# Weights rounded one block ahead in the heads, and the second block's attention values computed token-wise

## The reference

```python
# first block: 8 recurrent heads of 128 and 16 attention heads of 64
z = u @ w_in
hq, hf, hi, hg, aq, ak, av, gates = jnp.split(z, SPLIT_POINTS, axis=-1)
q = jax.nn.silu(hq) * (HG_DK ** -0.5)          # g = lb + (1 - lb) * sigmoid(hf)
o = rms_norm(hgrn2_scan(q, 1 - g, hi, log_g), hg_norm_w) * jax.nn.silu(hg)
ya = chunk_band_attention(aq, ak, av, rel_bias)
merged = gate_a * (y_a @ w_branch_a) + gate_b * (y_b @ w_branch_b)

# second block: 8 gMLP groups of 128 and 16 neighbourhood attention heads of 64
proj = h @ w_in
uv, qkv, gates = jnp.split(proj, [2 * GM_WIDTH, 2 * GM_WIDTH + 3 * NA_WIDTH], axis=-1)
y_a = gmlp_branch(uv, ln_g, ln_b, w_s, b_s)    # u * (w_s mixed over tokens of layernorm(gelu(v)) + b_s)
y_b = neighbourhood_attn(q, k, v, rpb)
```

## Time and profile before

| what | us |
|---|---|
| median of the runs | 2853.17 |
| the profiled execution | 2853.04 |
| its span in the trace | 2851.2 |
| TensorE busy in the span | 2815.1 (99%) |
| VectorE busy | 2162.9 (76%) |
| ScalarE busy | 1511.7 (53%) |
| GpSimd busy | 130.7 (5%) |
| moved by DMA | 521 MB, 183 GB/s over the span |

### The profile page before, as it was taken

How to read it: one execution, slowest core, us unless ns; L and a number is a source line. 1 busy time by engine, 2 the same in 40 slices (tenths; PEclk the granted TensorE clock), 3 DMA queues, 4 the chain that set the end, 5 groups by cost and what they waited for, 6 DMA issues and landing times.

```text
span 2851.2 us, 42194 instructions
## 1 busy us (share of the span) xinstructions
PE 2815.1 (99%) x16058; PEld 2422.3 (85%) x16058; DVE 2162.9 (76%) x3239; ACT 1511.7 (53%) x2248; POOL 130.7 (5%) x121
## 2 busy tenths in 40 slices
PE   9999999999999999999999999999999999999998
PEld 6888888888888888888888888888888888888887
DVE  5688877888777777777787766668768878777876
ACT  5555665656544444444465555546555555555554
POOL 0010000100100000000040000000010000000002
PEclk9999999999999999999999999999999999999999
DMA  7544554445555555555665565655556655555553
GB/s 267 180 146 153 167 160 156 157 159 184 192 190 192 184 193 186 188 193 183 194 213 189 172 192 161 197 174 186 189 180 190 196 190 187 190 192 187 189 188 123
DMA packets 157305, 521.23 MB, mean 183 GB/s; under 512 B 28976, under 2 KB 31408, under 8 KB 156976
## 3 DMA queue, kind: packets, MB, share of 16 engines
q1 hardware_dynamic: 155952, 516.26, 55.8%
q10 hardware_dynamic: 1152, 2.27, 0.2%
HBM read 516.37 MB, written 2.10 MB: 182 GB/s over the span
## 4 chain that ended last, share of the span: by engine, by line
PE 83%; DVE 11%; ACT 3%; issue 3%; DMA 0%; DVEq 0%; ACTq 0%; SPq 0%
PE acc L371 32%; PE acc L376 16%; PE psT L371 9%; PE psX L371 9%; PE psT L376 4%; PE psX L376 4%; DVE w_lo L1162 4%; ACT w_hi L733 2%; DVE HS L1303 1%; PE acc_first L371 1%; DVE work L1168 1%; DVE HS L1312 1%; PE acc L406 1%; PE acc L405 1%; PE acc L404 1%
## 5 line engine op out<-in xcount | busy, mean ns | idle before, releaser
L1162 DVE TENSOR_TENSOR w_lo<-w_raw,w_hi 128x1024 fp32r<-128x1024 f32 (+1 forms) x960 | 1171.1, 1226 | 368.1 <-ACT w_hi L733 342.1
L733 ACT ACTIVATE w_hi<-w_raw 128x1024 fp32r<-128x1024 f32 (+1 forms) x960 | 1000.4, 1052 | 435.2 <-PE acc L371 213.5
L371 PE MATMUL acc<-XU,w_hi 128*128 128x512 f32 x2784 | 904.5, 397 | 0.5 <-DVE work L1168 0.5
L371 PE MATMUL acc<-XY,w_hi 128*128 128x512 f32 x2208 | 715.4, 398 | 0.0
L376 PEld LDWEIGHTS acc<-XU,w_lo 128*128 128x128 f32 x2784 | 523.0, 188 | 121.7
L376 PE MATMUL acc<-XU,w_lo 128*128 128x256 f32 x2784 | 547.5, 278 | 0.0
L376 PEld LDWEIGHTS acc<-XY,w_lo 128*128 128x128 f32 x2208 | 414.9, 188 | 96.9 <-DVE XY L1350 1.1
L371 PEld LDWEIGHTS acc<-XU,w_hi 128*128 128x128 f32 x2784 | 436.0, 189 | 6.6 <-issue 2.7
L376 PE MATMUL acc<-XY,w_lo 128*128 128x256 f32 x2208 | 434.5, 278 | 0.8 <-DVE XY L1350 0.8
L371 PEld LDWEIGHTS acc<-XY,w_hi 128*128 128x128 f32 x2208 | 344.2, 189 | 8.6 <-issue 5.8
L738 ACT ACTIVATE cross<-acc 128x256 f32<-128x256 f32 x246 | 93.6, 380 | 238.1 <-PE acc L371 238.0
(11 more groups left out here) (295 smaller groups left out, 2972.0 us busy)
## 6 DMA issues: line engine op xcount, KB each, us to landing
w_raw<-in_weights SPq DMA_DIRECT2D x956, 512.0 KB, 3.5
bias<-in_rel_bias SPq DMA_DIRECT2D x8, 384.0 KB, 3.3
bias<-in_rpb_back SPq DMA_DIRECT2D x32, 96.0 KB, 6.7
w_raw<-in_weights SPq DMA_DIRECT2D x8, 384.0 KB, 3.0
hT<-in_x_t SPq DMA_DIRECT2D x8, 256.0 KB, 8.5
G<-in_norm_rows SPq DMA_DIRECT2D x1, 1024.0 KB, 7.6
out_dram<-G SPq DMA_DIRECT2D x2, 512.0 KB, 3.7
out_dram<-G ACTq DMA_DIRECT2D x2, 384.0 KB, 4.7
```

The source lines that it names most:

```text
L371: return nc.tensor.matmul(bank[:, :], hi[:, k, col:col + P], X[:, k0 + k, :], start=first and k == 0, stop=last and k == nk - 1 and k % 2 ...
L733: act.activation(w_hi[s][:, 0:n], w_raw[s][:, 0:n], ACT.Copy).then_inc(hi_done, 1)
L1162: V.tensor_tensor(w_lo[s][:, 0:n], w_raw[s][:, 0:n], w_hi[s][:, 0:n].bitcast(F32), ALU.subtract).then_inc(lo_ready, 1)
```

## The change

**Rounding.** In both head phases ACT rounds one block ahead of where its program stood: a new `round_next(p, i, b)` rounds what `round_block` for b+1 would (at the end of an iteration the next iteration's first, at the end of the phase nothing), and one `round_block(p, 0, 0)` stands ahead of the loop. In `heads1` it comes right after `copy_cross` in odd blocks, ahead of the block's job, and after the job in even blocks (at b = 0 first). In `heads2` it comes ahead of the jobs in all blocks.

**First heads.** DVE does `softmax_front` at b = 11 and 13 ahead of the tile sum and scaling of the gate tile, no longer behind them. PE does `attend` ahead of `scan_rms` at b = 17.

**Second heads.** The tile av goes out of the heads (14 blocks, 7 tiles); `gmv` has 32 blocks, of which the last 16 make av token-wise in the same banks. ACT copies it, scaled, in pieces of 128 columns to places of their own (`near_value`) at b = 23 and 31, four heads and two token tiles each, and raises `av_out`, for which PE waits at b = 0 and 2 of the first second head. The transposes L476 and the copy L1005 go. The layer-norm steps of the gate values move from the first second head into b = 16 to 21 of `gmv` (their squares now go to `probs`, gain and shift to the start of G). PE's jobs, and ACT's and DVE's steps for them, move up: mix to 5, scores to 6 and 8, transposes to 11, attend to 13. Seven tiles an iteration make bank and cross buffer alternate over iterations (`head2_bank`, `p.cross`). The bias is loaded at b = 4 in place of 6.

The diff, cut to its core (bodies of functions that only move are left out, and so are eight columns of indentation):

```diff
@@ -135,7 +135,7 @@
     ("ffn1last", 1, *ffn_counts("ffn1last"), None),
-    ("gmv", 1, 16, 0, 0, None), ("heads2", HEADS, 16, 8, 8, None),
+    ("gmv", 1, 32, 0, 0, None), ("heads2", HEADS, 14, 7, 7, None),
     ("branch2", 2, 16, 16, 16, None), ("out2", 2, 16, 8, 0, None),
@@ -225,13 +225,22 @@
 val_banks = [[acc[0], acc[1]], [psA, psE]]
-gain, shift = Gf[:, 16 * T:16 * T + WIDTH], Gf[:, 20 * T:20 * T + WIDTH]
+gain, shift = Gf[:, 0:WIDTH], Gf[:, WIDTH:2 * WIDTH]
...
     return G[:, KD + 2 * i + kind, :].rearrange("p (a n) -> p a n", a=NT)
+def near_value(i):
+    if i < 5:
+        return G[:, (8, 9, 12, 16, 20)[i], :].rearrange("p (a n) -> p a n", a=NT)
+    return (AT[:, 0:NT, :], v_nat[:, :, :], av_nat[:, :, :])[i - 5]
+def head2_bank(i, t):
+    return acc[(7 * i + t) % 2]
@@ -323,9 +332,9 @@
             sp.wait_ge(S("mz_ready1"), KD)
-            sp.dma_start(Gf[:, 16 * T:16 * T + 2 * WIDTH],
+            sp.dma_start(Gf[:, 0:2 * WIDTH],
                          bass.AP(tensor=norm_rows.tensor, offset=0, ap=[[0, P], [1, 2 * WIDTH]])).then_inc(S("bs_in"), 16)
-        if name == "heads2" and b == 6:
+        if name == "heads2" and b == 4:
             offset = i * (2 * RPB_R * RPB_C) + RPB_BACK
@@ -460,9 +469,9 @@
                 bank_free(p, i, t)
-            if p.name == "heads1" and i == 0 and b in (0, 2):
-                pe.wait_ge(S("vals_out"), NT * (3 + b // 2))
+            if i == 0 and b in (0, 2):
+                pe.wait_ge(S("vals_out" if p.name == "heads1" else "av_out"), NT * (1 + 2 * (p.name == "heads1") + b // 2))
             products(p, i, b, bank_of(t), X, KB * (b % 2), b % 2 == 0, b % 2 == 1)
@@ -541,8 +550,6 @@
             pe.wait_ge(S(f"probs_ready{x}"), i * 2 + 2)
-            if x == 2:
-                pe.wait_ge(S("av_ready2"), i + 1)
             for h, bank in enumerate((psT, psX)):
@@ -553,7 +560,7 @@
             pe.wait_ge(S(f"pT_ready{x}"), i * 3 + 3)
-            av = head_value(1, i) if x == 1 else av_nat[:, :, :]
+            av = head_value(1, i) if x == 1 else near_value(i)
             for h in range(2):
@@ -580,7 +587,7 @@
         16: [scan_out, prob_transposes(1)],
-        17: [scan_rms, attend(1)],
+        17: [attend(1), scan_rms],
     }
@@ -655,7 +662,10 @@
     for b in range(p.blocks):
-        value_products(p, b, XY, val_banks[b // (KD // 2)], one_by_one(x_ready, KD))
+        c = b // (KD // 2)
+        if b in (KD, 3 * KD // 2):
+            pe.wait_ge(S("gv_ready"), NT * (c - 1))
+        value_products(p, b, XY, val_banks[c % 2], one_by_one(x_ready, KD))
         if b == 3:
@@ -664,7 +674,6 @@
     pe.wait_ge(S("ws_in"), 16)
-    pe.wait_ge(S("gv_ready"), NT)
@@ -680,16 +689,15 @@
     after2 = {
-        6: [mix],
-        7: [scores(0, T, 2)],
-        8: [transpose_pair(wk(5), "avz_ready2", "avT_full2")],
-        9: [scores(1, T, 2)],
-        13: [prob_transposes(2)],
-        15: [attend(2)],
+        5: [mix],
+        6: [scores(0, T, 2)],
+        8: [scores(1, T, 2)],
+        11: [prob_transposes(2)],
+        13: [attend(2)],
     }
...
     for i in range(p.iters):
-        in_tiles(p, i, XY, after2, lambda t: acc[t % 2])
+        in_tiles(p, i, XY, after2, lambda t: head2_bank(i, t))
     branches("branch2")
@@ -735,7 +743,7 @@
         act.wait_ge(w_used, p.block(i, b) + 1)
-        act.activation(cross[:, c % 2, :], bank[:, T:2 * T], ACT.Copy).then_inc(cross_ready, 1)
+        act.activation(cross[:, p.cross(i, c) % 2, :], bank[:, T:2 * T], ACT.Copy).then_inc(cross_ready, 1)
@@ -796,7 +804,15 @@
                 value_tile(b // 8, a)
+    def round_next(p, i, b):
+        if b + 1 < p.blocks:
+            round_block(p, i, b + 1)
+        elif i + 1 < p.iters:
+            round_block(p, i + 1, 0)
     p = ph["heads1"]
+    round_block(p, 0, 0)
@@ -825,21 +841,25 @@
         for b in range(p.blocks):
-            round_block(p, i, b)
             t = b // 2
+            if b == 0:
+                round_next(p, i, b)
             if b % 2:
...
                 copy_cross(p, i, t, b, acc_first if t == 0 else acc[(t - 1) % 2])
+                round_next(p, i, b)
             if b == 1:
...
                 act.activation(wk(0), wk(0), ACT.Ln).then_inc(S("lg_ready"), 1)
+                round_next(p, i, b)
             if b == 3:
...
                 act.activation(lg_hi[:, :, :], psT[:, 0:T], ACT.Copy).then_inc(S("lg_hi_ready"), 1)
+                round_next(p, i, b)
             if b == 5:
@@ -958,6 +981,18 @@
+    def value_squares():
...
+    def value_rstd():
...
     p = ph["gmv"]
@@ -966,52 +1001,47 @@
-        if b % (KD // 2) == KD // 2 - 1:
+        if b == 17:
+            value_squares()
+        if b == 18:
+            value_rstd()
+        if b in (23, 31):
+            act.wait_ge(w_used, p.block(0, b) + 1)
+            for a in range(NT):
+                for h in range(4):
+                    ins = act.activation(near_value(4 * (c - 2) + h)[:, a, :], val_banks[c % 2][a][:, h * P:(h + 1) * P],
+                                         ACT.Copy, scale=tok_rs[:, a:a + 1])
+                ins.then_inc(S("av_out"), 1)
+        if b in (7, 15):
...
-    def value_squares():
...
-    def value_rstd():
...
+    round_block(p, 0, 0)
...
-            round_block(p, i, b)
...
-                copy_cross(p, i, t, b, acc[t % 2])
+                copy_cross(p, i, t, b, head2_bank(i, t))
+            round_next(p, i, b)
...
-            if i == 0 and b == 2:
-                value_squares()
-            if i == 0 and b == 3:
-                value_rstd()
...
-            if b == 8:
-                act.wait_ge(S("avT_full2"), i + 1)
-                act.activation(av_nat[:, :, :], psT[:, 0:T], ACT.Copy).then_inc(S("av_ready2"), 1)
...
+            if b == 11:
+                evac_pT(0, 2, i)
+            if b == 12:
+                evac_pT(1, 2, i)
...
-                evac_pT(0, 2, i)
-            if b == 14:
-                evac_pT(1, 2, i)
-            if b == 15:
@@ -1165,7 +1195,7 @@
         dve.wait_ge(cross_ready, p.cross(i, c) + 1)
-        mark(V.tensor_tensor(dst, bank[:, 0:T], cross[:, c % 2, :], ALU.add), acc_free,
+        mark(V.tensor_tensor(dst, bank[:, 0:T], cross[:, p.cross(i, c) % 2, :], ALU.add), acc_free,
              p.tile(i, t) + 1 + TILE_CREDIT)
@@ -1324,6 +1354,10 @@
                 low_part(p, i, b)
+            if b == 11:
+                softmax_front(0, P, 1, i)
+            if b == 13:
+                softmax_front(1, T, 1, i)
             if b in (11, 13, 15, 17):
@@ -1333,12 +1367,8 @@
                     link(ins)
-            if b == 11:
-                softmax_front(0, P, 1, i)
             if b == 12:
                 softmax_back(0, P, 1, i)
-            if b == 13:
-                softmax_front(1, T, 1, i)
             if b == 16:
@@ -1441,6 +1471,20 @@
+    def value_mean():
...
+    def centre_values(a):
...
+    def scale_values(a):
...
     p = ph["gmv"]
@@ -1448,22 +1492,14 @@
             norms_two()
-        for j in range(2 * b - KD, 2 * b - KD + 2) if b >= KD // 2 else ():
+        if b == 16:
+            value_mean()
+        if b in (18, 19):
+            centre_values(b - 18)
+        if b in (20, 21):
+            scale_values(b - 20)
+        for j in range(2 * b - KD, 2 * b - KD + 2) if KD // 2 <= b < KD else ():
             link(V.scalar_tensor_tensor(hT[:, j, :], hT[:, j, :], cols[:, C_FIN1 + j:C_FIN1 + j + 1], rs1[:, :], ALU.mult, ALU.mult))
-    def value_mean():
...
-    def centre_values(a):
...
-    def scale_values(a):
...
@@ -1472,14 +1508,7 @@
             t = b // 2
-            bank = acc[t % 2]
-            if i == 0 and b == 0:
-                value_mean()
-            if i == 0 and b == 3:
-                centre_values(0)
-                centre_values(1)
-            if i == 0 and b in (4, 5):
-                scale_values(b - 4)
+            bank = head2_bank(i, t)
             if b == 1:
@@ -1502,26 +1531,23 @@
             if b == 7:
-                scaled_tile(p, i, 3, b, 3, bank, wk(5), S("avz_ready2"), i + 1)
                 softmax_front(0, T, 2, i)
-            if b == 8:
-                softmax_back(0, T, 2, i)
             if b == 9:
-                tile_sum(p, i, 4, b, 4, bank, wk(8))
-                link(V.tensor_tensor(G[:, ds(i * 4, 1), :], work[:, 8:9, 0:T], rs[:, :].rearrange("p (a t) -> p a t", a=1), ALU.mult))
                 softmax_front(1, T, 2, i)
-            if b == 10:
-                softmax_back(1, T, 2, i)
-            if b in (11, 13, 15):
-                n = (b - 9) // 2
-                tile_sum(p, i, 4 + n, b, 4 + n, bank, wk(8))
+            if b in (7, 9, 11, 13):
+                n = (b - 7) // 2
+                tile_sum(p, i, 3 + n, b, 3 + n, bank, wk(8))
                 ins = V.tensor_tensor(G[:, ds(i * 4 + n, 1), :], work[:, 8:9, 0:T],
...
                     link(ins)
-            if b == 15:
+            if b == 8:
+                softmax_back(0, T, 2, i)
+            if b == 10:
```

(8 more changed lines are left out.)

30 lines of the change are left out of this document (16 added, 14 removed).

## The result

Before 2853.26 us (median of four runs), after **2828.94 us** (2827.18 to 2829.49, four runs): a ratio of 0.9914, 95% interval 0.9897 to 0.9931. That is 24.3 us less where 21.1 were forecast, and 0.06 us under the stated range, 2829 to 2840.

A forecast was written before the change was run, and what follows sets the result against it. TensorE, busy nearly all the time at full clock, was taken as the bound. From 2853.04 us, -17.3 + 1.0 - 1.1 - 1.9 - 1.8 = -21.1 gave 2831.9, 2832 us against the median; range 2829 to 2840.

The forecast's parts named there:

- Rival (3): First heads: DVE's late work is its own load, not ACT's order, so only -4.8 counts; 2848 us, chance 0.06.
- rival (4): First heads: ACT's new order starves the head start (sigmoids into logarithm and decays); 2853 us and over, chance 0.04.
- rival (2): First heads' tail: DVE stays the limit, block 16's bank or the square replaces old waits; 2840 to 2841, chance 0.10.
- -17.3 us for the two waits: First heads: TensorE's waits at `scan_rms` (8.9 us) and `scan_out` (8.4) both vanish; 0 to 0.3 us a head may remain.
- +1.0 us at `branch1`: Start of `branch1`: the 0.8 us wait for y_a's low part grows by 1.0 us (0 to 2.0).
- The cover at the head's tail: First heads' end: `AT_ready` at 216.7, before TensorE is ready at 217.45; square ready and asked for at 222.7, a tie.
- `gmv` and the second heads: -4.8 us: Second part of the change: token-wise blocks -1.1 us, dropped transposes -1.9, wait of `mix` gone -1.8.
- forecast -1.8: First `mix`: layer-norm statistics moved into `gmv` remove its 1.7 us wait and about 0.1 us of TensorE's restart.
- forecast 1.9: Second heads: the two transposes of the attention values go, 0.24 us a head, 1.9 us saved (1.0 to 3.0).
- The thin cover: Second heads: slack before scores and transposes falls to 0.3 us each, from 2.5 and 1.8; no new wait.
- Rival (1): Second heads: softmax front late from the copy behind the rounding, 0.5 to 1 us a head; 2836 to 2840, chance 0.12.
- The rule on table loads: y_a chain: skill's drain (2.8 us longer) or common Ln and Exp set (1.3 shorter); trace shows neither, sum uses neither.

The follow-up runs named there:

- round_alone: Kernel before with only ACT's rounding one block ahead in the first heads; 2833.23 us, ratio 0.9931.
- swap_alone: Kernel before with only `attend` put ahead of `scan_rms` at b=17 of the first heads; 2853.67 us, ratio 1.0002.
- front_alone: Kernel before with only DVE's `softmax_front` at b=11 and 13 ahead of the tile sum and scaling; 2846.25 us, ratio 0.9976.
- square_late_2: Changed kernel with `scan_rms` first at b=17, one early table load, and two idle DVE operations ahead of the square in each first head; 2828.53 us.
- square_late_3: Changed kernel with `scan_rms` first at b=17, one early table load, and three idle DVE operations ahead of the square in each first head; 2834.13 us.
- heads2_round_old: Changed kernel with the rounding back in its old place in the second heads only; 2842.41 us, ratio to the kernel before 0.9965.
- fronts_back: Changed kernel with `scan_rms` first at b=17, one early table load, and `softmax_front` back behind tile sum and scaling; 2824.26 us, ratio to before 0.9898.
- after_preload: Changed kernel with one explicit table load at b=17 of the first heads replacing separate loads for Ln and Exp; 2825.32 us, ratio to before 0.9904.
- stall_longer: Changed kernel with one more unused ACT copy of 1024 columns in the last first head's y_a chain; 2828.71 us.

## Why the prediction was right, and where it was wrong

**The mechanism was right.** ACT's order held back the rounding, that made DVE idle, and DVE's lateness made TensorE wait at `scan_out` and `scan_rms`. `round_alone` shows it by itself. Rival (3), that the edit doesn't reach the waits, and rival (4), slower, are out. So is rival (2): no bank and no square held TensorE up.

**The term that was mis-sized: -17.3 us for the two waits; it is -22.8.** The step that failed took a wait's cost from PE's idle row. The row counts from the modelled end of the matmul before, and what follows a wait starts more slowly: in the kernel before, `scan_out` and the transposes behind it took 1.45 us to the start of block 17, in the changed one 1.22. The trace had a better row, which the prediction did not use, the waits of the weight loads in the kernel before:

```profile
PEld psE L523 <- DVE work L1344: 11.4, 8, 1.4
PEld psE L517 <- DVE AT L1317: 10.7, 8, 1.4
```

11.4 + 10.7 = 22.1 us, against a measured 22.8. It holds for the experiments too; each stage against the same without the wait (482.5 us for `heads1`, 346.0 for `heads2`), with the rows' sums (the 10.2 of `front_alone` has its short rows at block 16, 0.14 us each):

| kernel | loss, us | PE's idle rows | PEld's rows |
|---|---|---|---|
| before | 22.8 | 17.3 | 22.1 |
| swap_alone | 20.8 | 14.2 | 20.7 |
| front_alone | 15.8 | 10.2 | 15.3 |
| square_late_2 | 3.5 | 1.3 | 3.8 |
| square_late_3 | 9.3 | 7.1 | 9.7 |
| heads2_round_old | 13.9 | 12.1 | 14.6 |

The loads' row was found after the losses were known, and no run was forecast with it. Wait by wait it is less exact than in the sums: in `swap_alone` it has 1.41 us at `scan_out`, 0.71 at the pair products and 0.55 at the square, where the blocks with these waits grew by 1.51, 0.58 and 0.38, and block 14 grew by 0.2 without a wait.

The forecast missed the measured time by less than this term: -5.5 us here and +1.9 at `branch1` (next) partly cancel, which is luck.

**The other mis-sized term: +1.0 us at `branch1`; it is +2.9.** The wait grew by 1.25 us as reasoned (the two table loads stand in the chain), which lies in the stated 0 to 2.0. What was not thought of is the clock. Windows of the changed kernel from the start of `branch1`:

```profile
582.40:588.40 6.00, 3.89 (x21) 2.94 (x20) 2.52 (x7) 4.92 (x8) 0.00 (x0) 1.00 0.31 101
588.40:592.30 3.90, 3.90 (x16) 3.37 (x15) 2.93 (x4) 2.77 (x5) 0.00 (x0) 0.56 0.43 134
```

In the second window the granted clock is 0.56 of full, between the levels 2.4 and 1.2 GHz: (1 - 0.56) / 0.5 * 3.9 = 3.4 us of it at 1.2 GHz. Block 1 takes 4.42 us instead of 2.87. Ahead of it TensorE had stood idle for 2.07 us. An idle time of 1.83 (`swap_alone`) and of 2.09 (`round_alone`) was followed by the same; one of 0.82 at the same place, and of 1.7 at `mix`, in the kernel before, was not. The Trainium skill, TensorE: Matmul & The Clock Gate, Part 1, has idleness take the clock to half, and the trace agrees. In the kernel before the clock was not full in the whole span, as was said of it, but as long as TensorE worked: it is 0.50 from 2844.1 us to the end.

**The cover at the head's tail was underestimated.** The forecast had the square in a tie with TensorE's asking, and `AT_ready` 0.75 us ahead; measured, the square is ready at 217.94 where it is asked for at 220.00, and `AT_ready` is 2.8 us ahead. The sum had kept the query product at 1.6 us, as in the kernel before, where POOL's key product had started first:

```profile
207.37 1.73 POOL L1113 TENSOR_TENSOR HS<-HS,work 128x512 f32<-128x512 f32 x1 [8.51 <-ACT HS L852]
```

DVE's started at 208.06, behind a low part, and took 1.59. In the changed kernel DVE's starts at 202.73, takes 0.69, and POOL's is the long one:

```profile
202.78 1.60 POOL L1143 TENSOR_TENSOR HS<-HS,work 128x512 f32<-128x512 f32 x1 [5.97 <-ACT HS L872]
```

The Trainium skill, SBUF — State Buffer, section "Who interferes with whom", has the two engines share a pair of ports by an exclusive lock, so that the order of starting decides who stands; both rows agree. That is 0.9 us of the 2.1 by which `AT_ready` was earlier than forecast. The rest is that DVE enters the stretch earlier, which the prediction named and left out of its sum: its low part of b=11 starts 3.6 us earlier than in the kernel before (198.03 against 201.62), TensorE's `scan_out` is reached only 2.4 us earlier. With this slack `attend` first and the early `softmax_front` are superfluous (`round_alone`, `fronts_back`); the prediction had worked them into its ready times.

**`gmv` and the second heads: -4.8 us, as forecast, term by term.** Token-wise blocks 2.72 us; the block with the first `mix` 3.60 instead of 5.54 (-1.9, forecast -1.8, of which 0.1 for the restart came from no row); the transposes 0.13 us in one block and 0.10 in the next, 1.8 in all (forecast 1.9). The thin cover held. The third second head, DVE and then PE, answering:

```profile
1676.49 0.42 DVE L1527 TENSOR_TENSOR XU<-work,XU 128x256 fp32r<-128x256 f32 x1 [1.75 <-ACT XU L1035]
...
1680.19 0.69 DVE L1266 TENSOR_REDUCE soft<-probs 128x2 f32<-128x512 f32 x1
...
1689.78 0.36 DVE L1273 TENSOR_SCALAR probs<-probs,soft 128x256 f32<-128x256 f32 x1
...
1681.28 0.48 PE L543 MATMUL psS<-work 64*128 64x256 f32 x1
...
1690.39 0.60 PE L555 MATMUL psT<-ident,probs 128*128 128x128 f32 x4
```

DVE idles 1.75 us behind y_a's copy (forecast 1.5), scores read at 1680.88, asked for at 1681.28: 0.4 us of slack (forecast 0.3). Probabilities at 1690.13, asked for at 1690.39: 0.26 (forecast 0.3). Rival (1) is out. But the prediction took this edit for a cost of the second heads; `heads2_round_old` shows that the rounding ahead is what the 14 blocks stand on, at exponentials and transposes.

**The range.** It was made from the waits' idle rows as an upper end of the gain, so nothing in it reached beyond 24 us; its lower end as worked out there (no +1.0, transposes at 3.0) is 2829.8, and 2829 was stated. The load rows, 22.1 us in place of 17.3, would have put the sum at 2832 - 4.8 = 2827 without the clock and 2829 with it.

**The rule on table loads.** `after_preload` takes the load between Ln and Exp away and the chain is 1.28 us shorter. That Ln and Exp share a set, as the Trainium skill has it (ScalarE: Activation LUTs, section "Table sets: the hidden batching unit"), is so here; the loads that were there before were placed all the same, one for each. A drain behind a load is not seen in the changed kernel either: the load at 220.66 ends at 221.94 and Ln starts at 221.95.

What stays open: why the share beside the idle row differs between places (0.08 to 0.42 us), and why block 14 grew in `swap_alone`. Moving the layer-norm steps and the token-wise values were not tried one by one; their prices are read from the blocks.

## What to carry to other kernels

Price the waits of a stage by the idle time of TensorE's weight loads, not by that of its matmuls: in six kernels their sum was within 9% of what the waits cost, where the matmuls' rows missed 13 to 63%. It doesn't hold the cost of the clock: at the start of `branch1` in the changed kernel the loads' row has 2.4 us, and the stage was 4.2 us longer than without a wait. Before spending effort on the instruction that TensorE waits for, ask whose order makes it late; reordering TensorE's own jobs only moved the wait (`swap_alone`), while letting ACT do the pipeline's work ahead of a job that waits took it all. And when a stall moves to a single place, look at the clock behind it: this idle time of 2.1 us cost 2.1 us more than itself, 1.5 of them in the slow block behind it.

## What was unexpected of the hardware

- After an idle time of TensorE of 1.8 to 2.1 us its granted clock was at 1.2 GHz for 3.4 us. With 3.0 us of idle time (`stall_longer`) the half level was on from the first matmul behind it and the loss beside the idle time was 1.8 us in place of 2.1.
- ACT runs Exp with the table set that was loaded for Ln; one explicit load replaced two, 1.28 us.
- DVE's product of 512 columns takes 0.69 us when it starts ahead of POOL's, and took 1.59 when it started behind it.
